# TensorE adds five modulation tiles of the first block and four of each later one; x is loaded behind the first tile; ScalarE issues the small loads

## The reference, cut to what matters

```python
cond = jax.nn.silu(c)                                   # c: one vector of 2048
for layer in range(2):
    mod = cond @ ada_w[layer] + ada_b[layer]            # ada_w[layer]: 2048 x 6144
    shift, scale, gate = jnp.split(mod, 3, axis=-1)
    h = rms_norm(x, norm_w[layer]) * (1.0 + scale) + shift
    y = branch(h)                                       # in-projection, mixer, out-projection
    x = x + gate * y
```

## Time and profile before

| | |
|---|---|
| median of 3 runs | 1510.47 us (1510.14 to 1512.03) |
| profiled execution, its own time | 1509.85 us |
| its span, first to last instruction | 1508.1 us |
| TensorE busy | 1446.5 us, 96% |
| VectorE busy | 1105.2 us, 73% |
| first granule's first matmul | 44.08 us |
| sums of blocks 0, 1, 2, 3 begin | 38.82, 79.01, 118.12, 162.53 us |

### The profile page before, as it was taken

One profiled execution on the slowest core, in us unless ns is written; L12 is line 12 of the kernel. 1 busy time (PEld: TensorE's weight loads), 2 busy tenths in 40 slices (PEclk: granted clock), 3 DMA queues, 4 the chain that ended last, 5 costly groups with the idle time before them and its releaser, 6 DMA issues.

```text
span 1508.1 us, 19057 instructions
## 1 busy us (share of the span) xinstructions
PE 1446.5 (96%) x6679; PEld 1198.7 (79%) x6679; DVE 1105.2 (73%) x1234; ACT 744.5 (49%) x1002; POOL 41.7 (3%) x78
## 2 busy tenths in 40 slices
PE   2889999999999989899999999999999999999998
PEld 2767888888888867688888888888888888888886
DVE  5999899989898875878766566566566666656657
ACT  3544646454446455544544544544554454554452
POOL 1000110101000000000000000000000000000000
PEclk9999999999999999999999999999999999999999
DMA  9999889998989735798766566556566566566553
GB/s 338 386 393 391 269 282 339 324 327 287 336 294 353 263 114 183 254 310 300 251 184 187 174 191 185 173 189 188 174 194 181 173 191 193 167 189 190 178 182 112
DMA packets 199230, 361.47 MB, mean 240 GB/s; under 512 B 14224, under 2 KB 48360, under 8 KB 199164
## 3 DMA queue, kind: packets, MB, share of 16 engines
q1 hardware_dynamic: 198112, 359.60, 72.3%
q10 hardware_dynamic: 1056, 1.06, 0.2%
HBM read 358.51 MB, written 2.11 MB: 239 GB/s over the span
## 4 chain that ended last, share of the span: by engine, by line
PE 76%; issue 10%; DVE 7%; ACT 3%; DMA 2%; SPq 1%; POOL 0%; ACTq 0%; DVEq 0%; POOLq 0%
PE proj L1336 23%; PE proj L1338 22%; PE proj L1337 22%; DVE ada_acc L853 4%; PE mix L1336 1%; PE mix L1338 1%; PE mix L1337 1%; DVE w_lo L834 1%; DMA raw<-in_att_w_in 1%; DMA ada_more<-in_ada_w 1%; ACT w_hi L563 1%; PE mix L1455 1%; PE mix L1522 1%; PE mix L1570 1%; ACT work L646 1%
## 5 line engine op out<-in xcount | busy, mean ns | idle before, releaser
L834 DVE TENSOR_TENSOR w_lo<-raw,w_hi 128x1024 fp32r<-128x1024 f32 x480 | 585.5, 1222 | 355.5 <-ACT w_hi L563 354.8
L563 ACT ACTIVATE w_hi<-raw 128x1024 fp32r<-128x1024 f32 x480 | 507.4, 1061 | 682.5 <-PE proj L1338 570.5
L1336 PE MATMUL proj<-w_hi,h_hi 128*128 128x512 f32 x1472 | 583.7, 397 | 7.1 <-DVE h_lo L906 3.9
L1338 PE MATMUL proj<-w_hi,h_lo 128*128 128x512 f32 x1472 | 575.2, 391 | 0.0
L1337 PE MATMUL proj<-w_lo,h_hi 128*128 128x512 f32 x1472 | 574.6, 390 | 0.0
L1336 PEld LDWEIGHTS proj<-w_hi,h_hi 128*128 128x128 f32 x1472 | 277.7, 189 | 66.9 <-issue 9.1
L1338 PEld LDWEIGHTS proj<-w_hi,h_lo 128*128 128x128 f32 x1472 | 277.1, 188 | 58.6
L1337 PEld LDWEIGHTS proj<-w_lo,h_hi 128*128 128x128 f32 x1472 | 277.7, 189 | 57.6 <-issue 1.4
L853 DVE SCALAR_TENSOR_TENSOR ada_acc<-ada_raw,cond,ada_acc 128x1024 f32<-128x1024 f32 x148 | 188.9, 1276 | 2.8 <-DMA ada_raw<-in_ada_w 1.8
L1336 PE MATMUL proj<-w_hi,y_hi 128*128 128x512 f32 x320 | 126.0, 394 | 1.3 <-DVE stream L1004 1.3
L1338 PE MATMUL proj<-w_hi,y_lo 128*128 128x512 f32 x320 | 124.6, 389 | 0.0
(11 more groups left out here) (202 smaller groups left out, 936.5 us busy)
## 6 DMA issues: line engine op xcount, KB each, us to landing
raw<-in_mlstm_w_in SPq DMA_DIRECT2D x192, 512.0 KB, 3.7
ada_raw<-in_ada_w SPq DMA_DIRECT2D x160, 512.0 KB, 6.0
raw<-in_att_w_in SPq DMA_DIRECT2D x128, 512.0 KB, 7.1
raw<-in_mlstm_w_in SPq DMA_DIRECT2D x128, 256.0 KB, 3.0
raw<-in_mlstm_w_out SPq DMA_DIRECT2D x64, 512.0 KB, 4.3
raw<-in_att_w_out SPq DMA_DIRECT2D x32, 512.0 KB, 6.1
ada_more<-in_ada_w SPq DMA_DIRECT2D x16, 512.0 KB, 10.9
work<-in_ada_w SPq DMA_DIRECT2D x16, 512.0 KB, 10.6
```

The costliest lines, as they stand in the source:

```text
L563: act.activation(w_hi[:, c % LEAD, :], raw[:, c % LEAD, :], ACT.Copy).then_inc(hi_ready, 1)
L834: dve.tensor_tensor(w_lo[:, c % LEAD, :], raw[:, c % LEAD, :], w_hi[:, c % LEAD, :].bitcast(F32), ALU.subtract).then_inc(lo_ready, 1)
L1336: pe.matmul(out_, a_hi, b_hi, start=start, stop=False, **kw)
L1338: return pe.matmul(out_, a_lo, b_hi, start=False, stop=stop, **kw)
```

## The change

It has four parts. (1) TensorE computes some tiles of a block directly, with the tile as weights and `cond[:, t]` as moving column, adding up in `mix[3]` on top of what VectorE has summed: tiles 3, 5, 8, 14, 15 of block 0 and 12 to 15 of blocks 1, 2, 3 (17 tiles). VectorE leaves these out. (2) The slot of such a tile is free only when TensorE has done it, so that SP waits for TensorE there (`slot_free`). (3) x is loaded right behind tile 0, with a semaphore for each chunk, and VectorE's norm steps come at tiles 2 and 4 in place of 9 and 11, the copy of the small weights at tile 0 in place of 8. (4) ScalarE issues the five small loads.

```diff
+        BY_PE = {0: (3, 5, 8, 14, 15), 1: (12, 13, 14, 15), 2: (12, 13, 14, 15), 3: (12, 13, 14, 15)}
+        def by_pe(n):
+            return n % KT in BY_PE.get(n // KT, ())
+        def taken(n):
+            return sum(not by_pe(i) for i in range(n))
+        def turned(n):
+            return sum(by_pe(i) and i % KT < KT - 1 for i in range(n))
...
+        def slot_free(sp, n):
+            if by_pe(n) and n % KT == KT - 1:
+                sp.wait_ge(ada_summed, n // KT + 1)
+            elif by_pe(n):
+                sp.wait_ge(ada_pe, turned(n + 1))
+            else:
+                sp.wait_ge(ada_tile, taken(n + 1))
...
-            wait(sp, ada_tile, n + 1 - (ADA_START if n < ADA_LATE + ADA_SLOTS else ADA_SLOTS))
+            before = n - (ADA_START if n < ADA_LATE + ADA_SLOTS else ADA_SLOTS)
+            if before >= 0:
+                slot_free(sp, before)
...
         def sp_program(sp):
-            sp.dma_start(rows_c, c[0].rearrange("(t p) -> t p", p=P)).then_inc(c_in, 16)
-            sp.dma_start(const[:], consts[:, 0:C_COS]).then_inc(consts_in, 16)
-            sp.dma_start(rows_n, norm_w.rearrange("l (t p) -> (l t) p", p=P)).then_inc(c_in, 16)
+            load_ada(sp, 0)
             sp.wait_ge(bias_zeroed, 1)
-            for n in range(KT):
+            sp.dma_start(ada_bias[0:1], ada_rows[0:1, 0:2, 0:NC]).then_inc(ada_bias_in, 16)
+            for q in range(CHUNKS):
+                sp.dma_start(stream[:, :, q * NC:(q + 1) * NC], x_v[:, :, q * NC:(q + 1) * NC]).then_inc(x_in[q], 16)
+            for n in range(1, KT):
                 load_ada(sp, n)
-                if n == 3:
-                    sp.dma_start(rows_v, mlstm_norm_w[0].rearrange("(t p) -> t p", p=P)).then_inc(rows_in, 16)
-                    sp.dma_start(conv_rows, mlstm_conv_w[0]).then_inc(rows_in, 16)
-                for q in X_AFTER.get(n, []):
-                    sp.dma_start(stream[:, :, q * NC:(q + 1) * NC], x_v[:, :, q * NC:(q + 1) * NC]).then_inc(x_in, 16)
...
         def squares(act, layer, q):
             if layer == 0:
-                act.wait_ge(x_in, 16 * CHUNKS)
+                act.wait_ge(x_in[q], 16)
...
         def turn_bank(layer, q):
-            return mix[q % 4] if layer or q < 4 else proj[q // 2 % 2][q % 2]
+            if layer:
+                return mix[q % 4]
+            return [mix[0], mix[1], mix[2], proj[1][1], proj[0][0], proj[0][1], proj[1][0], mix[0]][q]
...
         def act_program(act):
+            act.dma_start(rows_c, c[0].rearrange("(t p) -> t p", p=P)).then_inc(c_in, 16)
+            act.dma_start(const[:], consts[:, 0:C_COS]).then_inc(consts_in, 16)
+            act.dma_start(rows_n, norm_w.rearrange("l (t p) -> (l t) p", p=P)).then_inc(c_in, 16)
+            act.dma_start(rows_v, mlstm_norm_w[0].rearrange("(t p) -> t p", p=P)).then_inc(rows_in, 16)
+            act.dma_start(conv_rows, mlstm_conv_w[0]).then_inc(rows_in, 16)
...
             for n in range(KT):
-                take_ada(dve, n)
-                if n == 8:
+                if not by_pe(n):
+                    take_ada(dve, n)
+                if n == 0:
...
-                if n == 9:
+                if n == 2:
                     norm_sum(dve, 0)
-                if n == 11:
+                if n == 4:
                     norm_scale(dve, 0)
...
+        def mod_part(pe, k, t, first=False):
+            n = k * KT + t
+            pe.wait_ge(ada_in[slot_of(n)], slot_fills(n) * 16)
             for j in range(8):
+                op = pe.matmul(mix[3][:, j:j + 1], ada_slot[slot_of(n)][:, j // 4, j % 4 * P:(j % 4 + 1) * P],
+                               cond[:, t:t + 1], start=first and j == 0, stop=t == KT - 1 and j == 7)
+            if t < KT - 1:
+                op.then_inc(ada_pe, 1)
+            else:
+                op.then_inc(ada_summed, 1)
+        def mod_taken(pe, k, first):
+            pe.wait_ge(ada_tile, taken(k * KT + KT))
+            last = not by_pe(k * KT + KT - 1)
+            for j in range(8):
+                op = pe.matmul(mix[3][:, j:j + 1], ada_acc[:, k % 2, j // 4, j % 4 * P:(j % 4 + 1) * P],
+                               ones[:, 0:1], start=first and j == 0, stop=last and j == 7)
+            if last:
+                op.then_inc(ada_summed, 1)
+        def mod_sum(pe, k):
+            mod_taken(pe, k, True)
+            for t in BY_PE.get(k, ()):
+                mod_part(pe, k, t)
...
             pe.wait_ge(cond_ready, 1)
+            mod_part(pe, 0, 3, True)
+            mod_part(pe, 0, 5)
             pe.wait_ge(xn_act, CHUNKS)
             pe.wait_ge(xn_dve, CHUNKS)
-            for q in range(UNIT):
+            for q in range(4):
                 turn_x(pe, 0, q)
-            pe.wait_ge(xnT_act, 4)
-            mod_sum(pe, 3, 0, 0)
+            mod_part(pe, 0, 8)
+            for q in range(4, UNIT):
+                turn_x(pe, 0, q)
+            mod_part(pe, 0, 14)
+            mod_taken(pe, 0, False)
+            mod_part(pe, 0, 15)
             pe.wait_ge(xnT_act, UNIT)
```

More of the change, by code:

```diff
@@ L289, in build @@
             "consts_in", "rows_in", "norms_in", "gates_in"))
-        x_in, x_again, ones_set, rows_turned = (sem(n) for n in (
-            "x_in", "x_again", "ones_set", "rows_turned"))
+        x_again, ones_set, rows_turned = (sem(n) for n in ("x_again", "ones_set", "rows_turned"))
+        x_in = [ctx.enter_context(nc.semaphore(f"x_in{q}")) for q in range(CHUNKS)]
         cond_ready, rows_out, masks_ready, rope_table = (sem(n) for n in (
@@ L332, in build @@
         v1_hi_ready, pT1_hi_ready = (sem(n) for n in ("v1_hi_ready", "pT1_hi_ready"))
-        c_in, conv_turned, norm_turned = (sem(n) for n in ("c_in", "conv_turned", "norm_turned"))
+        c_in, conv_turned, norm_turned, ada_pe = (sem(n) for n in ("c_in", "conv_turned", "norm_turned", "ada_pe"))
         raw_in = [ctx.enter_context(nc.semaphore(f"raw_in{i}")) for i in range(LEAD)]
@@ L483, in load_ada @@
                 [slice(2, 3), slice(b * 2 * NC, (b + 1) * 2 * NC)]
-            if n % KT == 0:
-                wait(sp, ada_tile, n - KT + 1)
+            if n and n % KT == 0:
+                wait(sp, ada_tile, taken(n - KT + 1))
                 bias = ada_bias[0:1] if kind == MOD else ada_bias[0:1].rearrange("p s n -> p (s n)")
                 sp.dma_start(bias, ada_rows[layer:layer + 1, cols[0], cols[1]]).then_inc(ada_bias_in, 16)
-            wait(sp, ada_tile, n + 1 - (ADA_START if n < ADA_LATE + ADA_SLOTS else ADA_SLOTS))
+            before = n - (ADA_START if n < ADA_LATE + ADA_SLOTS else ADA_SLOTS)
+            if before >= 0:
+                slot_free(sp, before)
             dst = ada_slot[slot_of(n)]
@@ L533, in sp_program @@
                 if i == X_AGAIN:
-                    sp.wait_ge(ada_tile, ADA_GATE1)
+                    sp.wait_ge(ada_tile, taken(ADA_GATE1))
                     for q in range(CHUNKS):
@@ L842, in take_ada @@
             if t:
-                dve.wait_ge(ada_tile, n)
+                dve.wait_ge(ada_tile, taken(n))
                 other = sum_
@@ L1231, in dve_program @@
                 {i + 1: [lambda k=k: mod_evac(dve, 3, k, 1, k - 4)] for i, k in SUM_MOD1.items()},
-                {i: [lambda n=n: take_ada(dve, n) for n in ns] for i, ns in TAKES0.items()},
+                {i: [lambda n=n: take_ada(dve, n) for n in ns if not by_pe(n)] for i, ns in TAKES0.items()},
                 {-4: [lambda: h_rest(dve, 0, 1)]},
@@ L1439, in turn_x @@
             pe.wait_ge(xn_dve, CHUNKS * layer + q // 2 + 1)
+            if layer == 0 and q == 7:
+                pe.wait_ge(xnT_act, 1)
             if layer and q >= 4:
@@ L1449, in turn_x @@
             op.then_inc(ht_done, 1)
-        def mod_sum(pe, bank, k, which):
-            pe.wait_ge(ada_tile, k * KT + KT)
+        def mod_part(pe, k, t, first=False):
+            n = k * KT + t
+            pe.wait_ge(ada_in[slot_of(n)], slot_fills(n) * 16)
             for j in range(8):
-                op = pe.matmul(mix[bank][:, j:j + 1], ada_acc[:, which, j // 4, j % 4 * P:(j % 4 + 1) * P],
-                               ones[:, 0:1], start=True, stop=True)
-            op.then_inc(ada_summed, 1)
+                op = pe.matmul(mix[3][:, j:j + 1], ada_slot[slot_of(n)][:, j // 4, j % 4 * P:(j % 4 + 1) * P],
[16 more added lines that the diff above has]
+                mod_part(pe, k, t)
         def gate_sum(pe, bank, b):
             first = (ADA_GATE0 if b < CHUNKS else ADA_GATE1) // KT
-            pe.wait_ge(ada_tile, (first + b % CHUNKS // 2 + 1) * KT)
+            pe.wait_ge(ada_tile, taken((first + b % CHUNKS // 2 + 1) * KT))
             op = pe.matmul(mix[bank][:], ones[:], ada_acc[:, b // 2 % 2, b % 2, :], start=True, stop=True)
@@ L1625, in pe_program @@
             layer0 = merged(
-                {i: [lambda i=i, k=k: sum_behind(pe, *sum_free[i], mod_sum, 3, k, k % 2)]
+                {i: [lambda i=i, k=k: sum_behind(pe, *sum_free[i], mod_sum, k)]
```

1 line of the change is left out of this document (removed).

## The result

The changed kernel takes 1542.74 us (median of 4 runs, 1540.44 to 1546.74) against 1510.51 us (1510.14 to 1512.03) for the kernel before on the same chip: ratio 1.0214, 95% interval 1.0202 to 1.0226. It is slower, as forecast, but by 32.2 us where 22.5 were forecast. The profiled execution has a span of 1538.8 us, 30.7 more than before.

The account below looks back on a forecast made before the run. TensorE, busy 96% of the span, was taken as the bound, with transfers pacing the opening. Terms -5.1 - 7.1 + 20.6 + 12.6 + 4.5 - 3.0 = +22.5 us on 1510.47 gave 1533 us, range 1513 to 1540.

Parts of the forecast that it names:

- +20.6: Sums of blocks 1 to 3: twelve tiles computed on TensorE at 1.72 us each add 20.6 us.
- +12.6: Sums 1 to 3: the clock falls inside each 8.6 us sum, doubling its last 4.2 us; +12.6 us for three.
- The rule that I had weighed against the trace: Weight loads in the sums: time is columns over 1.2 GHz whatever the clock, making the forecast 12.6 us less.
- VectorE's relief: Blocks 1 to 3: VectorE loses 12 takes, so TensorE's waits of 2.08, 2.06 and 2.91 us vanish; -7.1 us.
- the slow granules behind: Granules right behind sums 1 to 3 run at the low clock, 1.5 us a sum; +4.5 us.
- The 3.0 us that before lost in the same way: Behind sums 1 and 2: the earlier kernel's slow-clock loss of 1.5 us each goes; -3.0 us.
- the opening: Up to the first granule: early x and small loads start it at 39.0 in place of 44.08 us; -5.1 us.
- my other end of 43.5 us: Late bound for the first granule's start, forecast at 38.4 to 43.5 us, with low clock costing up to 5 us.
- The clock did not hold: Rival for the later sums: one-column matmuls keep 2.4 GHz; +5.4 us, 1516 us; chance 0.14.
- the loads did slow: Rival for the later sums: weight loads take 0.107 us at either clock; +9.9 us, 1520 us; chance 0.12.
- SP starving TensorE: Rival for blocks 1 to 3: SP's slot waits delay transfers some 3 us a block; 1542 us; chance 0.10.
- what I named to look for: Trace signs: x squared 9 to 13 us, clock 0.5 inside sums, sum 3 ending some 20 us later, same work behind.

Follow-up runs that it names:

- e9: Kernel before plus early x and ScalarE's small loads, no tiles computed on TensorE; each sum of blocks 1 to 3 computed five times: 1550.38 us, ratio 1.0254.
- e3: Changed kernel with TensorE computing tiles only in blocks 1 to 3, block 0 wholly on VectorE: 1539.48 us, ratio 1.0195.
- e11: Changed kernel plus three dense float32 matmuls in front of the opening's first tile on TensorE: 1541.87 us, ratio 1.0212.
- e6: Changed kernel with TensorE computing only tiles 14 and 15 of blocks 1 to 3, none in block 0: 1521.18 us, ratio 1.0059.
- e4: Changed kernel with TensorE's tiles of each later block spread behind two or three neighbouring granules: 1548.84 us, ratio 1.0245.
- e8: Changed kernel with TensorE computing only tiles 3, 5 and 8 of block 0, none in later blocks: 1509.44 us, ratio 0.9995.
- e1: Changed kernel with all 64 tiles back on VectorE; early x, earlier norm steps and ScalarE's small loads stay: 1509.83 us, ratio 0.9995.
- e10: Kernel before with only the five small loads issued by ScalarE: 1510.38 us, ratio 0.9999.
- e2: Changed kernel with TensorE computing only block 0's tiles 3, 5, 8, 14, 15; blocks 1 to 3 on VectorE: 1510.34 us, ratio 1.0002.
- e12: Same kernel as e2, run again on another chip for a second trace: 1513.91 us, ratio 1.0025.
- e7: Changed kernel, TensorE's tiles only in blocks 1 to 3, spread over two or three granules, VectorE's and ScalarE's steps moved along: 1539.76 us, ratio 1.0183.

## Why the prediction was right or wrong

**Right: the direction, and what the later sums cost.** The terms +20.6 and +12.6 make 33.2 us; the three sums took 38.68 - 5.49 = 33.2 us more. The mechanism is the forecast one: the clock falls inside a run of one-column matmuls, and their weight loads slow with it, 3.41 us for 16 against 1.70. The rule that I had weighed against the trace for those loads (the Trainium skill, TensorE: Matmul & The Clock Gate, section LDWEIGHTS (loading the stationary operand)) would have made the sums 12.6 us shorter; 0.21 us a load over hundreds of them now stands against it. e9 shows that these instructions are enough.

The size is in part luck. I had put the fall 4.4 us into each sum, the mean of two falls in the trace of before, and in the changed kernel it came after 4.5, 3.5 and 5.2 us, mean 4.4. But e3 and e11 have the same pieces in the same places, and their three sums took 40.25 and 37.97 us; in e6 the clock fell after 3.9, 2.7 and 2.8 us. Where it falls varies by 3 us, so that agreement to the tenth is chance and only the size is shown.

**Right: VectorE's relief,** -7.1 us forecast, 7.85 - 0.99 = 6.9 measured. VectorE did wait for `shift_c`, 11.30 us at sum 2, at no cost to TensorE in this kernel; in e4, with 17.60 us, it did cost:

```profile
139.47 0.16 DVE L890 COPY shift_c<-mix 128x4 f32<-128x4 f32 x1 [11.30 <-PE mix L1490]
```

**Nearly right: the slow granules behind,** +4.5 forecast, about 5.7 measured: 2.55 us behind sum 1 (12 matmuls in 5.27 us where 12 at 0.227 take 2.72), about 1.65 and 1.5 behind the others. The 3.0 us that before lost in the same way went.

**Wrong: the opening, -5.1 forecast, +3.3 measured.** This is the step that failed, 8.4 us. I priced its six pieces at 1.72 us, "near the quick end, since the recorded clock is 0.97 in the opening", and set them against the arrival of the tiles. They took 3.4 to 3.5 us each, so TensorE's own row of work, 27.2 us from 17.86 on, became the path in place of the tiles. Even my other end of 43.5 us was short, since it let the low clock slow only the last three pieces, for 5 us, with the first three hidden ahead of the tiles; it slowed all six, 6 x 1.7 = 10. With +3.3 in place of -5.1 the sum is +30.9 us and the forecast 1541.4, against 1542.74 measured. e11 shows the clock as the cause of the pace, e8 that without parts 14 and 15 the granules start 6.3 us earlier.

The change also took away what had brought the clock up in the kernel before. There 32 transpose instructions stand in one row:

```profile
32.99 3.65 PE L1447 MATMUL mix<-const,work 128*128 128x128 f32 x16 [16.20 <-ACT work L583]
36.43 2.55 PE L1447 MATMUL proj<-const,work 128*128 128x128 f32 x16
```

The first 16 take 36.43 - 32.99 = 3.44 us, the others 38.82 - 36.43 = 2.39, and the sum behind them runs at full speed. e1, with its 32 in a row too, speeds up likewise. In the changed kernel, and in e8, parts 3 and 5 stand in front of them and part 8 between the halves, and each half takes 3.4 to 3.5 us; the forecast of 6.2 us for all of them came from the rows of before, and they took 6.9.

The rest of the error is smaller. Tile 3, which started TensorE's row, was there at 17.86 us where my working has 12.2 + 3 x 1.34 = 16.2. With the pieces at the pitch of the earlier trace rows, 3.4 us each, and the rest as forecast, the working would have given 16.2 + 6 x 3.4 + 6.2 + 2.2 = 45.0 us for the first granule, +0.9 us; the late tile and the slower transposes are the other 2.4. And beneath that the term was too hopeful: e1 finds 0.75 us at the first granule for the early x and the small loads without parts, as VectorE's takes start late behind it; e10 finds 1.1 us for the small loads, which I had counted at 2.2; and e1, e8 and e10 find that 0.75 to 3 us gained there do not reach the end.

**The rivals.** The clock did not hold, and the loads did slow. SP starving TensorE would have given 1542, near the measured time, by another way. SP's wait for TensorE in the changed kernel, 47 to 200 us (waited for: us in total, times, longest):

```profile
SPq L519 <- PE mix L1490: 31.4, 8, 9.8
```

SP was held for up to 9.8 us behind TensorE's parts, and the DMA share fell to 0.89; but TensorE was idle for 0.99 us in all, so the wait did not reach it, and e9 is slow without this wait. The match in time is a coincidence.

**Of what I named to look for:** x was squared at 9.2 to 14.8 us (9 to 13 forecast); sum 3 ended 29.9 us later than before, not 20; the groups at each sum, the clock, TensorE's idle time and the stretch behind came as named.

## What to carry to other kernels

Work moved to TensorE is priced by its time there and by what it does to the clock. Here one piece with dense work right in front cost its 1.7 us and no more (sum 3 in before, e1, e2, e8, e10 and e12). From two pieces on, the clock fell inside them or up to 1 us behind them in every case but the two groups at sum 3 of e4; from there a piece costs twice as much, and the dense work behind slows too. Price work in an opening at the low clock unless the trace shows the pitch of the high one, and look at what brings the clock up there before taking it apart. To relieve an engine that is not the bound is worth only the waits it causes (here 7 us), and it is paid for in full on the engine that is.

## What the runs showed of the hardware

- The recorded clock is 1.00 from the start up to the first change on record, whatever the clock is. In the changed kernel six pieces ran at 0.21 us an instruction at a recorded 1.00, and the first granule's matmuls at 0.43 us; e11 ran the same piece at the same pace at a recorded 0.50. The pitch of a known instruction tells more.
- The clock fell with TensorE busy for 100% of the time (2.00 of 2.00 us in each window from 82 to 86 us). A busy share of one-column work did not keep it. With two to five pieces in a row and no idle time in front, it fell 2.4 us (e7, sum 2) to 5.5 us (e11, sum 3) after the first of them began; only at sum 3 of e4 did it not fall.
- Float32 transposes in a row did bring the clock up: 3.44 us for the first 16 instructions of before, 2.39 for the next 16.
- In the opening, 27.2 us of one-column work and transposes without a gap never brought the clock up in the changed kernel, while in e8 the dense matmuls from 41.05 us on had it back at about 47 us (0.43 us each, then 0.23).
- The same order of pieces and granules kept the clock at sum 3 in e4, and lost it twice at sum 2 of e4 and twice at sum 3 of e7. What differs between them was not found.
